# A hybrid decoder layer: x copied once in quarters, its squares summed by TensorE, gates in column groups, 512-wide memory keys

## The reference, cut to what matters

```
def rms_norm(x, g):
    y = xf * lax.rsqrt(jnp.mean(xf * xf, axis=-1, keepdims=True) + EPS)
    return (y * g).astype(x.dtype)

mn = rms_norm(mem, norm_mem)
k = rms_norm((mn @ wk).reshape(B, N_MEM, X_HEADS, X_HD), k_norm)   # memory keys, 512 columns
h = rms_norm(x, p['norm_mix'])
proj = h @ p['w_in']      # 4360 columns: mLSTM q, k, v, o, gates (8 columns), attention q, k, v
```

## Time and profile before

| | |
|---|---|
| median of the timed runs | 1355.51 us |
| profiled execution | 1354.58 us |
| its span | 1352.8 us, granted clock 1.00 |
| TensorE busy | 1327.7 us, 98% |
| VectorE busy | 818.2 us, 60% |
| ScalarE busy | 620.9 us, 46% |
| GpSimd busy | 98.6 us, 7% |
| first matmul | 7.81 us |
| weight stream | 388 chunks of 512 KB, 3.5 us from issue to landing (median) |

### The profile page before, as it was taken

How to read it: one execution, slowest core, us unless ns; L and a number is a source line. 1 busy time by engine, 2 the same in 40 slices (tenths; PEclk the granted TensorE clock), 3 DMA queues, 4 the chain that set the end, 5 groups by cost and what they waited for, 6 DMA issues and landing times.

```text
span 1352.8 us, 27266 instructions
## 1 busy us (share of the span) xinstructions
PE 1327.7 (98%) x10213; PEld 1299.8 (96%) x10213; DVE 818.2 (60%) x1240; ACT 620.9 (46%) x889; POOL 98.6 (7%) x140
## 2 busy tenths in 40 slices
PE   7999999999999997999999999999999999999999
PEld 7998989988999987999999999999999999999999
DVE  7767888888756456656444556444565444565443
ACT  7674666666534456443333344333344333343331
POOL 0031001111523203000000000000000000000000
PEclk9999999999999999999999999999999999999999
DMA  9687445675955953654545555554555554555553
GB/s 380 254 228 253 134 140 184 193 232 166 368 180 158 299 203 110 218 158 156 183 159 166 167 161 155 178 164 160 168 164 159 171 170 156 169 158 168 171 160 127
DMA packets 75420, 251.87 MB, mean 186 GB/s; under 512 B 8348, under 2 KB 17392, under 8 KB 74704
## 3 DMA queue, kind: packets, MB, share of 16 engines
q1 hardware_dynamic: 59184, 215.49, 48.4%
q0 software_dynamic: 15888, 35.07, 8.4%
q10 hardware_dynamic: 288, 0.48, 0.1%
HBM read 238.00 MB, written 13.63 MB: 186 GB/s over the span
## 4 chain that ended last, share of the span: by engine, by line
PE 86%; DVE 6%; ACT 4%; issue 2%; DMA 2%; SPq 0%; DVEq 0%; ACTq 0%
PE g L521 81%; PE m L521 3%; DMA raw<-in_stream 2%; ACT arena L997 2%; DVE wlo L1476 1%; DVE arena L1462 1%; ACT whi L1015 1%; DVE arena L1459 1%; DVE b_lo L1462 0%; ACT a_hi L997 0%; DMA arena<-in_memT 0%; DVE arena L1451 0%; DVE arena L1455 0%; DVE small L1742 0%; PE m L746 0%
## 5 line engine op out<-in xcount | busy, mean ns | idle before, releaser
L1476 DVE TENSOR_TENSOR wlo<-raw,whi 128x1024 fp32r<-128x1024 f32 x388 | 475.5, 1235 | 371.4 <-ACT whi L1015 359.9
L1015 ACT ACTIVATE whi<-raw 128x1024 fp32r<-128x1024 f32 x388 | 407.4, 1058 | 471.3 <-PE g L521 440.7
L521 PE MATMUL g<-a_hi,whi 128*128 128x288 f32 x1632 | 353.5, 298 | 1.5 <-ACT a_hi L997 1.5
L521 PE MATMUL g<-a_hi,wlo 128*128 128x288 f32 x1632 | 350.2, 296 | 0.0
L521 PE MATMUL g<-a_lo,whi 128*128 128x288 f32 x1632 | 348.7, 295 | 0.0
L521 PE MATMUL g<-b_hi,whi 128*128 128x288 f32 x1344 | 287.8, 295 | 5.5 <-DVE arena L1459 5.3
L521 PE MATMUL g<-b_hi,wlo 128*128 128x288 f32 x1344 | 289.0, 296 | 0.0
L521 PE MATMUL g<-b_lo,whi 128*128 128x288 f32 x1344 | 287.0, 295 | 0.0
L521 PEld LDWEIGHTS g<-a_hi,whi 128*128 128x128 f32 x1632 | 261.7, 188 | 7.6 <-issue 4.0
L521 PEld LDWEIGHTS g<-a_lo,whi 128*128 128x128 f32 x1632 | 261.9, 188 | 0.0
L521 PEld LDWEIGHTS g<-a_hi,wlo 128*128 128x128 f32 x1632 | 261.5, 188 | 0.0
(11 more groups left out here) (181 smaller groups left out, 690.9 us busy)
## 6 DMA issues: line engine op xcount, KB each, us to landing
raw<-in_stream SPq DMA_DIRECT2D x388, 512.0 KB, 3.5
arena<-in_state_C POOLq DMA_DIRECT2D x8, 512.0 KB, 5.8
out_s_C<-arena POOLq DMA_DIRECT2D x8, 512.0 KB, 3.5
arena<-in_kdT POOLq DMA_DIRECT2D x8, 512.0 KB, 15.0
arena<-in_cache_mem_v POOLq DMA_DIRECT2D x8, 512.0 KB, 8.7
arena<-in_xT SPq DMA_DIRECT2D x4, 576.0 KB, 8.4
arena<-in_memT SPq DMA_DIRECT2D x4, 512.0 KB, 7.0
arena<-in_x_prompt SPq DMA_DIRECT2D x2, 1024.0 KB, 10.0
```

The costliest lines, as they stand in the source:

```text
L521: return pe.matmul(out, lhsT, rhs, start=start, stop=stop, skip_group_check=True)
L1015: act.activation(whi[:, s], raw[:, s], ACT.Copy).then_inc(sem["hi_done"], 1)
L1476: dve.tensor_tensor(wlo[:, s], raw[:, s], f32(whi[:, s]), SUB).then_inc(sem["chunk_split"], 1)
```

## The change

- SyncE: chunk 0 is copied in two halves, the memory in six pieces of two contraction tiles and one of four, x once, in quarters behind chunks 6, 7, 9 and 10. The copies `xtok` and `xdec` go, and a wait for the split memory with them.
- The memory keys' chunks hold 2 contraction tiles by 512 columns instead of 4 by 256; 12 matmuls of 512 columns a chunk, both token halves in their own PSUM bank. The keys are copied out in round 10, by four copies.
- Four matmuls on zeros run on TensorE before the first chunk.
- The squares of x are taken elementwise from xT, three of eight pieces by GpSimd and five by ScalarE (rounds 8 to 11), and summed over the features by 16 full-precision matmuls against ones in four column groups (`x_sums`, after chunk 12); ScalarE copies the four partial sums and `norm_x` (now after chunk 13) adds them up.
- The gates: 16 full-precision matmuls of the scaled gate weights with xT, in four column groups (after chunk 11), a copy by ScalarE, and two matmuls that add the groups up (`gates_sum`, after chunk 12). VectorE's `gates_a` has two products and two sums fewer.
- `x_prep` moves from rounds 2 to 9 to rounds 5 to 11, and gates, key norm and key turn move one or two rounds later.

```
-        for kt in range(12, KT):
-            beside[0].append(("mem_prep", kt))
+        for kt in range(6, KT):
+            beside[kt // 2 - 3].append(("mem_prep", kt))
         for kt in range(KT):
-            beside[2 + kt // 2].append(("x_prep", kt))
-        beside[7].append(("gate_weights",))
-        for j in range(3):
-            beside[10 + j].append(("x_squares", j))
-        for c, what in ((12, "norm_x"), (12, "gates_mm"), (13, "gates_a"), (14, "gates_ln"), (15, "gates_b"),
-                        (16, "gates_c"), (17, "keys_turn"), (17, "gates_exp"), (19, "keys_rev"), (20, "columns"),
+            beside[(5, 5, 6, 6, 7, 7, 8, 8, 8, 9, 9, 9, 10, 10, 10, 11)[kt]].append(("x_prep", kt))
+        beside[9].append(("gate_weights",))
+        for j in range(8):
+            beside[(6, 6, 7, 8, 9, 10, 11, 11)[j]].append(("x_squares", j))
+        for c, what in ((11, "gates_mm"), (12, "x_sums"), (12, "gates_sum"), (13, "norm_x"), (14, "gates_a"), (15, "gates_ln"),
+                        (16, "gates_b"), (17, "gates_c"), (18, "keys_turn"), (18, "gates_exp"), (20, "keys_rev"), (21, "columns"),
...
-        beside[15].append(("k_norm",))
+        beside[17].append(("k_norm",))
...
+            def warm():
+                pe.wait_ge(sem["dve_once"], before["warm_ready"] + 1)
+                for _ in range(4):
+                    mm(M[3][:, 0:256], rstd[:, 0:P], rstd[:, 0:256])
+
+            def mem_chunk(c):
...
+                    for i, (w, a) in enumerate(((whi, act_hi[1]), (whi, act_lo[1]), (wlo, act_hi[1]))):
...
+                        for j in range(2):
+                            m = mm(G[2 + j][:, :], a[:, kt, j * P:(j + 1) * P],
+                                   w[:, s, 2 * k:2 * k + 2, :].rearrange("p a b -> p (a b)"), kt == 0 and i == 0,
+                                   kt == KT - 1 and i == 2)
...
             def norm_x():
+                pe.wait_ge(sem["act_once"], before["ssum_out"] + 1)
+                mm(M[0][:, 0:NT], ones, ssum).then_inc(sem["pe_once"], 1)
+
+            def x_sums():
...
+                for k in range(4):
+                    for i in range(4):
+                        m = mm(M[0][32 * i:32 * i + 32, 0:NT], ones[:, 0:32], xq2[2 * k + i // 2][:, i % 2, :], k == 0, k == 3)
...
             def gates_mm():
-                for kt in range(KT):
-                    half, k = divmod(kt, 8)
-                    w = wgx[:, half, MH * k:MH * k + P]
-                    for i, a in enumerate((act_hi, act_lo)):
-                        m = mm(M[1][:, 0:NT], w, a[0][:, kt, :], kt == 0 and i == 0, kt == KT - 1 and i == 1)
+                for k in range(4):
+                    for i in range(4):
+                        m = mm(M[1][32 * i:32 * i + 32, 0:NT], wgs[:, 4 * k + i, :], xT[:, 4 * k + i, :], k == 0, k == 3)
...
+            def gates_sum():
+                pe.wait_ge(sem["act_once"], before["gsum_out"] + 1)
+                mm(M[2][0:32, 0:NT], cst[:, C_SEL:C_SEL + 32], gsum)
+                mm(M[2][32:64, 0:NT], cst[:, C_SEL + MH:C_SEL + MH + 32], gsum).then_inc(sem["pe_once"], 1)
...
-                if c % 4 == 3 and c // 4 != KVA or c == 4 * KVA + 4:
+                if c == 4 * KVA + 2:
+                    for j in range(2):
...
+                        for half in range(2):
+                            copy(kvm[:, j, half * CW:(half + 1) * CW],
+                                 G[2 + j][:, half * CW:(half + 1) * CW]).then_inc(sem["tile_out"], 1)
+                            dve.wait_ge(sem["tile_out"], now("tile_out"))
+                elif c > 4 * KVA and c % 4 == 3 and c // 4 != KVA or c == 4 * KVA + 5:
```

More of the change, by code:

```diff
@@ L142, in weight_stream @@
     every = range(0, D, CK * P)
-    out = tiles(w["wk_x"][0], every, range(0, XW, CW))
+    out = [w["wk_x"][0][r:r + 2 * P].reshape(2, P, 2, CW).transpose(0, 2, 1, 3).reshape(CK * P, CW)
+           for r in range(0, D, 2 * P)]
     out += tiles(w["w_in"][0], every, (COL_KA,))
@@ L186, in gate_columns @@
 def gate_columns(w_in):
[L188 to L191, removed]
+    return w_in[0][:, COL_G:COL_G + 2 * MH].reshape(KT, P, 2 * MH).transpose(1, 0, 2)
 ARENA = 18500
@@ L372, in load, with mem @@
                 sp.dma_start(dst, src).then_inc(signal, 16)
-            for b in range(4):
+            def mem(b):
+                kt = slice(2 * b, 2 * b + 2 if b < 6 else KT)
+                load(memT[:, kt, :], ins["memT"][:, kt, :], sem["mem_in"][b])
+            half = 2 * CW
+            load(raw[:, 0, 0:2].rearrange("p a b -> p (a b)"), ins["stream"][0][:, 0:half], sem["raw_ready"][0])
+            mem(0)
+            load(raw[:, 0, 2:4].rearrange("p a b -> p (a b)"), ins["stream"][0][:, half:2 * half], sem["first_raw"])
@@ L376, in _, with x_load @@
+            for b in range(1, 4):
                 chunk(b, ins["stream"][b], None)
-                load(memT[:, CK * b:CK * b + CK, :], ins["memT"][:, CK * b:CK * b + CK, :], sem["mem_in"][b])
-            for b in range(4):
-                chunk(b, ins["stream"][RING + b], b + 1)
+                mem(b)
+            mem(4)
+            def x_load(b):
                 load(xT[:, CK * b:CK * b + CK, :], ins["xT"][:, CK * b:CK * b + CK, :], sem["x_in"][b])
-                if b == 1:
-                    load(wg_raw[:, :, :], ins["gates"], sem["wg_in"])
@@ L383, in _ @@
[L383 to L393, removed]
+            for c in range(RING, 4 * RING):
+                chunk(c % RING, ins["stream"][c], c - RING + 1)
+                if c < 6:
+                    mem(c + 1)
+                if c in X_AFTER:
+                    x_load(X_AFTER.index(c))
+                if c == 7:
+                    load(wg_raw[:, :, :], ins["gates"], sem["wg_in"])
+                if c == 11:
@@ L531, in chunk @@
                 s = c % RING
-                if first and t + 1 >= GB:
+                if first and t > 2 * KVA:
                     pe.wait_ge(sem["tile_out"], more_t + (t + 2 - GB))
@@ L1937, in _ @@
                         g, t = G[(2 * q + j) % GB], 2 * q + j
-                        if q < KVA:
-                            copy(kvm[:, j, q * CW:(q + 1) * CW], g[:, 0:CW]).then_inc(sem["tile_out"], 1)
-                            dve.wait_ge(sem["tile_out"], now("tile_out"))
-                        elif QKM <= q < OM and (q - QKM) % 2 == 0:
+                        if QKM <= q < OM and (q - QKM) % 2 == 0:
                             ct = q - QKM + j
@@ L2188, in add_square @@
                 pool.wait_ge(sem["sq_sum"], now("sq_sum"))
+            pool.wait_ge(sem["mem_hi"], 7)
+            pool.wait_ge(sem["mem_lo"], 7)
+            for j in range(3):
+                pool.wait_ge(sem["x_in"][j // 2], 16)
+                x = xT[:, 2 * j:2 * j + 2, :]
+                pool.tensor_tensor(xq2[j], x, x, ALU.mult).then_inc(sem["x_add"], 1)
+                pool.wait_ge(sem["x_add"], now("x_add"))
             pool.wait_ge(sem["act_once"], before["gate_rows"] + 1)
```

141 lines of the change are left out of this document (86 added, 55 removed).

## The result

The changed kernel is slower: 1363.62 us median (1362.39 to 1365.01), the kernel before beside it 1355.20 (1354.57 to 1355.52); ratio 1.0066, 95% interval 1.0053 to 1.0078. The forecast was 1358.7, with a range up to 1362: the direction is as forecast, the size is not.

The account below looks back on a forecast made before the run. TensorE, busy 98%, bounds the kernel, with VectorE only just in time; after the change VectorE's queue limits. Gain of 1.3 us by chunk 14, then a 4.5 us stall at the turn: +3.2, median 1358.7, own range 1356 to 1361.5.

Parts of the forecast that it names:

- Keys of 512 columns: Key matmuls on TensorE: 0.239 us each at worst, 0.213 at best; a gain of 1.0 us was taken.
- The start: First key matmul on TensorE: near 5.45 us instead of 7.81, 2.4 earlier, because the first copy is half a chunk.
- x tile 15 is ready at 44.6 (42.7 to 46.5): Last x tile, needed by chunk 11: VectorE's queue makes it ready at 44.6 us, using up TensorE's earlier gain.
- VectorE's work of 36.9 us: VectorE's queue before x tile 15: subtractions, key and x tiles, memory keys' eviction and gate weights sum to 36.9 us.
- start and chunk 1: VectorE's waits before x tile 15: 0.55 us for chunk 1 and 0.3 for handovers.
- chunk 7: VectorE's wait for chunk 7 before x tile 15: 0.9 to 2.2 us, taken as 1.5.
- GpSimd beside it: GpSimd's three squares beside VectorE: 0 to 2.2 us more, most of it inside the wait, taken as 0.4.
- the term 4.5: TensorE's stall at the key turn, waiting for VectorE's key product: 4.5 us, bounds 1.6 to 5.5.
- the clock falls in the new gap: Rival, chance 0.16: after the stall at the turn TensorE runs at half rate, costing 1.75 us more: 1360.5.
- TensorE was the only limit: Rival, chance 0.11: VectorE has slack in rounds 9 to 11 and at the turn, all 6.7 us stay gained: 1348.8.
- only one of the two limits holds: Rival, chance 0.16: only VectorE's late x tile 15 (1354.2) or only the stall at the turn (1353.3) holds.
- Column groups don't overlap: Rival, chance 0.02: gate and square matmuls run as 32 at 0.4 us instead of 8 rounds, 8.7 more: 1367.

Follow-up runs that it names:

- the version without warming: The kernel of "all edits with one copy" without the four warming matmuls before the first key matmul: 1351.50 us, ratio 0.9978.
- all edits with one copy: Changed kernel with later eviction, squares and last x quarter, early DRAM copies, key norm in round 15, gate weights moved, chunk 0 in one copy: 1352.18 us.
- the key's norm first: Changed kernel with the key's norm ahead of the gates' third part in VectorE's round 17: 1360.00 us, ratio 1.0038.

## Why the prediction was right or wrong

*Right.* The direction, and the two places that it named: waits inside chunks 9 to 11 that end with VectorE's x preparation, and a wait at the turn, behind the gates' third part on VectorE. Keys of 512 columns take 0.231 us at full rate (a pair each 0.46), where 0.239 was the worst and 0.213 the best case: 0.8 us, taken as 1.0. Gates 2.08, squares and the gates' sum 2.55, norm 0.27: 4.9, taken as 5.3. No wait in front of the norm. The start gained 1.9 of 2.4. The keys did not end near 28.2, though, but at 30.63: in spite of the warming, the first twelve key matmuls took some 0.44 us each. As VectorE sets the pace behind them, this did not decide the total; the version without warming is level with the one with it.

*The step that failed: "x tile 15 is ready at 44.6 (42.7 to 46.5)".* It was ready at 48.54, and at 47.2 at the earliest in the traces without an edit in front of it, outside the range in all. VectorE's work of 36.9 us in front of it was right; the waits and stretches were not:

| term | prediction | trace |
|---|---|---|
| start and chunk 1 | 0.55 + 0.3 | 0.30 + 1.13 + 1.37 = 2.80 |
| chunk 7 | 1.5 | 0 (0.21 for chunk 6) |
| GpSimd beside it | 0.4 | (2.66 - 1.00) + (2.05 - 1.23) = 2.48 |
| chunk 11's copy, ScalarE's rounds | 0 | 0.64 + 0.61 + 0.17 = 1.42 |
| sum | 2.75 | 6.91 |

The sum is 4.2 us over, and VectorE started 0.2 earlier: 48.6. Two terms were mis-sized by 2 us each: GpSimd's squares beside VectorE, which did not fall into a wait for chunk 7 as assumed, since there was none; and the waits for chunk 0's second half and chunk 1. The terms aren't to be had one by one. Without GpSimd's squares, 1.4 us of waits for chunks 7 and 8 come back and chunk 11 is waited for 1.5 (VectorE's idle time in that run), so that at most 0.8 is left; with ScalarE's squares, gate weights, the last copy of x and the eviction out of the way as well, the tile is 3.6 earlier. What the prediction lacked was the order of limits behind VectorE: the copies at some 408 GB/s (10 to 30 us), and ScalarE with 3.38 us a round (1.06, 1.66 and 0.69, each starting just before the last one ends) once squares stand in each.

*The turn: the term 4.5 measured 3.4.* From the norm's matmul to the transposes 20.45 us, not 21.7. Its rival "the clock falls in the new gap", given a chance of 0.16, came true as well, at 1.5 us for the 1.75 it was priced at; the two were not alternatives but came together.

*Not foreseen: the decode scores, 2.7 us more of wait.* The half rate behind it (1.5 us) is made up by two shorter waits further on. The prediction carried the lateness of 3.2 through to the end unchanged. It had no row of the 88 to 125 us in it and did not follow the gates' output into GpSimd's queue, where two copies of 2 MB stand behind it. From 94 to 124 us the DMA engines are full (381 GB/s), chunk 32 lands 10.2 us after its issue instead of 7.3, and early copies take the wait away.

In sum, for the profiled executions: 3.2 forecast, + 4.1 for the tile, - 1.3 for the turn's chain, + 1.5 for the clock, + 2.7 at the decode scores gives 10.2; the spans differ by 10.0. The right direction came out of misses of both signs, then, and the 4.1 is that of one execution.

*Rivals.* "TensorE was the only limit" and "only one of the two limits holds" are out by the waits. "Column groups don't overlap" is out: 32 records in 2.15 us.

*Left open.* Why two halves make the copies slower from 4 to 6 us; the copies are issued 0.47 us apart either way. Whether one copy is worth a microsecond in the times. Why the same waits lower the clock in one execution and not in another. How much of the 8.4 us between the medians falls to each of the three places: the traces give one execution each.

## What to carry to other kernels

Price a moved step by everything that its output releases, on GpSimd's and SyncE's queues too, and follow that to the next stretch in which the DMA engines are full. A wait on TensorE that is long enough to show the clock falling is paid twice; so take the order of VectorE's work at such a wait as part of the change, which here meant one line. And where an engine is said to set a time, name the limit behind it before pricing what is taken off it: 2.5 us came off VectorE and 0.8 at most were kept.

## What the runs showed of the hardware

- The clock falls, from 2.4 to 1.2 GHz, behind waits that differ. At the turn it fell behind 3.38 or 3.39 us in all six traces with such a wait (0.63 to 0.82 granted in the 5 us after 80), and not behind 1.38. At the decode scores it fell behind 2.60, 2.97 and 3.17, and not behind 0.95 to 1.52. At the wait for chunk 1, at some 11 us, it fell in four traces with 1.88 to 2.67 (0.66 to 0.74 granted from 10 to 15 us), and not in three with 1.52 to 1.73. Behind 1.15 and 2.0 with 2.6 us of work between it fell in three traces (gates 3.84, 3.74, 3.19 us) and not in three (2.15). And behind 0.88 in front of the decode probabilities it fell in two traces (all edits with one copy; the key's norm first) of the ten with that wait. What a wait costs is therefore not fixed: 1.3 to 2.7 us more behind the same 3.4 (16.95 to 18.30 from the turn to the query sums, where 15.6 is the time without).
- Warming: after 3.62 to 3.78 us of matmuls on zeros the first pair of key matmuls took 1.19 us with 0.15, 0.61 and 0.75 us of idle time between, 0.70 to 0.74 with 0.28 to 0.56, and 0.71 with 1.19 and 1.26: the idle time does not decide it. The granted clock of the window from 5 to 10 us reads 1.00 either way.
- GpSimd's squares of 576 columns from SBUF stretch VectorE's two-operand work from 1.00 to 2.66 and from 1.23 to 2.05 us, more than its additions in the earlier trace rows did; with the squares moved away both are back at 1.00 and 1.23.
